# Forgetting attention by pairs of heads, with one 128 by 128 turn for each pair and block

## What is computed

```python
def forgetting_attention(q, k, v, f_logit, b_f):
    ...
    log_f = jax.nn.log_sigmoid(f_logit.astype(jnp.float32) + b_f.astype(jnp.float32))
    c = jnp.cumsum(log_f, axis=1).transpose(0, 2, 1)
    ...
    for blk in range(S // Q_BLOCK):
        q0, q1 = blk * Q_BLOCK, (blk + 1) * Q_BLOCK
        logits = jnp.einsum('bqhd,bkhd->bhqk', q[:, q0:q1], k[:, :q1]).astype(jnp.float32) * scale
        logits = logits + c[:, :, q0:q1, None] - c[:, :, None, :q1]
        ...
        p = jax.nn.softmax(logits, axis=-1)
        outs.append(jnp.einsum('bhqk,bkhd->bqhd', p.astype(v.dtype), v[:, :q1]))
```

## Time and profile before

| | |
|---|---|
| median of 3 runs | 3592.46 us |
| lowest and highest | 3590.16 and 3597.49 us |
| span of the profiled execution, first to last instruction | 3589.3 us |
| the profiled execution's own time, beside its span | not recorded; the lowest run is 0.9 us above the span |
| mean granted clock of TensorE | 0.997 of full speed |
| PE busy | 3512.9 us, 98% |
| PEld busy | 2764.4 us, 77% |
| DVE busy | 1567.7 us, 44% |
| ACT busy | 1279.2 us, 36% |
| POOL busy | 443.6 us, 12% |
| first score matmul of the stage of the change | 257.53 us |
| first matmul of the next stage on real data | 327.79 us |

### The profile page before, as it was taken

The page is one execution under the profiler, slowest core; times in us unless marked ns, Lnnn a source line. Parts: engine busy times, 40 slices in busy tenths (PEclk is TensorE's granted clock), DMA queues, the critical chain, the costliest instruction groups (busy, mean ns, idle before and its releaser), DMA issues. The chain is left out here.

```text
span 3589.3 us, 41664 instructions
## 1 busy us (share of the span) xinstructions
PE 3512.9 (98%) x15716; PEld 2764.4 (77%) x15740; DVE 1567.7 (44%) x2129; ACT 1279.2 (36%) x1792; POOL 443.6 (12%) x366
## 2 busy tenths in 40 slices
PE   9999999999999999999999999999999999999998
PEld 7787788877778886888875688877888875688886
DVE  3386433356643334333375733335333255733335
ACT  4343422245542324332333533235332333533324
POOL 0001111000111101221000022102221000022102
PEclk9999999999999999999999999999999999999999
DMA  4201233222123322333220233313333220133322
GB/s 146 87 1 36 81 95 110 96 71 71 38 80 99 105 95 65 95 100 105 84 64 15 71 96 97 112 61 98 100 94 109 79 78 18 53 94 99 111 71 76
DMA packets 78029, 292.06 MB, mean 81 GB/s; under 512 B 8656, under 2 KB 11472, under 8 KB 77648
## 3 DMA queue, kind: packets, MB, share of 16 engines
q1 hardware_dynamic: 77328, 289.31, 25.4%
q10 hardware_dynamic: 576, 1.05, 0.1%
HBM read 288.22 MB, written 2.10 MB: 81 GB/s over the span
## 5 line engine op out<-in xcount | busy, mean ns | idle before, releaser
L157 DVE TENSOR_TENSOR w_low<-w_raw,w_high 128x1024 fp32r<-128x1024 f32 (+4 forms) x513 | 672.6, 1311 | 1520.1 <-ACT w_high L152 1520.0
L191 PE MATMUL bank<-x_high,w_high 128*128 128x512 f32 x2856 | 1119.2, 392 | 21.0 <-DVE w_low L157 9.2
L193 PE MATMUL bank<-x_high,w_low 128*128 128x512 f32 x2856 | 1111.5, 389 | 0.0
L192 PE MATMUL bank<-x_low,w_high 128*128 128x512 f32 x2856 | 1111.4, 389 | 0.0
L152 ACT CAST w_high<-w_raw 128x1024 fp32r<-128x1024 f32 (+4 forms) x513 | 555.0, 1082 | 842.5 <-PE bank L193 835.4
L191 PEld LDWEIGHTS bank<-x_high,w_high 128*128 128x128 f32 x2856 | 536.2, 188 | 147.2 <-DVE w_low L157 14.3
L193 PEld LDWEIGHTS bank<-x_high,w_low 128*128 128x128 f32 x2856 | 536.1, 188 | 112.3
L192 PEld LDWEIGHTS bank<-x_low,w_high 128*128 128x128 f32 x2856 | 536.4, 188 | 111.2 <-issue 1.7
L191 PE MATMUL bank<-hidden_high,w_high 128*128 128x512 f32 x1056 | 410.8, 389 | 0.0
L192 PE MATMUL bank<-hidden_low,w_high 128*128 128x512 f32 x1056 | 410.8, 389 | 0.0
L193 PE MATMUL bank<-hidden_high,w_low 128*128 128x512 f32 x1056 | 410.8, 389 | 0.0
(11 more groups left out here) (537 smaller groups left out, 3432.5 us busy)
## 6 DMA issues: line engine op xcount, KB each, us to landing
w_raw<-in_stream SPq DMA_DIRECT2D x381, 512.0 KB, 3.5
w_raw<-in_stream SPq DMA_DIRECT2D x96, 704.0 KB, 4.0
w_raw<-in_stream SPq DMA_DIRECT2D x16, 384.0 KB, 3.1
w_raw<-in_stream SPq DMA_DIRECT2D x4, 576.0 KB, 3.7
dft_positions<-in_dft SPq DMA_DIRECT2D x2, 1024.0 KB, 4.8
w_raw<-in_stream SPq DMA_DIRECT2D x16, 128.0 KB, 2.1
out<-result SPq DMA_DIRECT2D x4, 512.0 KB, 2.7
h<-in_x ACTq DMA_DIRECT2D x4, 256.0 KB, 6.2
```

The lines of the kernel that those rows point to most:

```text
L157: self.nc.vector.tensor_tensor(self.lo[:, j % 2, 0:size], self.raw[:, j % RAW_SLOTS, 0:size], self.hi[:, j % 2, 0:size].bitcast(F32), ALU. ...
L191: nc.tensor.matmul(out, lhs[0], rhs[0], start=start, stop=False)
L192: nc.tensor.matmul(out, lhs[0], rhs[1], start=False, stop=False)
L193: return nc.tensor.matmul(out, lhs[1], rhs[0], start=False, stop=stop)
```

## The change

The units are put in another order and the turn is cut into smaller ones. `per` is 128 / 64 = 2 heads. The outer loop goes over pairs of heads, the next over blocks, and the inner one over the two heads of the pair. So units 0 and 1 have 512 keys, 2 and 3 have 384, 4 and 5 have 256, 6 and 7 have 128, and unit 8 starts again with 512 for the next pair of heads. After each second unit the 128 finished columns are turned by one transpose and copied by one ACT instruction of 128 by 128. That makes 16 turns of one transpose and 16 copies in place of 4 turns of four transposes and 4 copies.

`o_rows` shrinks from 2 x 512 to 2 x 128 columns. Turns 0 and 1 and all odd ones go to bank 6, the even ones from turn 2 on to bank 7. Since the first turn comes in iteration 4, the side task's logarithm and exponential go from ACT's iteration 4 to 3, PE waits for the logarithm in iteration 4 in place of 10, ahead of that iteration's scores, and it waits for DVE's multiplication in iteration 8.

```diff
--- before.py
+++ after.py
@@ -1462,8 +1462,13 @@
 
 
     blocks = range(NB - 1, -1, -1) if causal else range(NB)
-    units = [(qb, h) for qb in blocks for h in range(heads)]
+    per = P // width
+    units = [(qb, h) for first in range(0, heads, per) for qb in blocks for h in range(first, first + per)]
     n_units = len(units)
+
+    def turned_bank(i):
+
+        return C.bank[7 if i >= 2 and i % 2 == 0 else 6]
 
     def keys(n):
         return (units[n][0] + 1) * P if causal else T
@@ -1473,7 +1478,7 @@
             return ctx.enter_context(sbuf(nc, name, shape, F32))
         probs = sb("probs", [P, 2, T])
         probs_t = sb("probs_t", [P, 2, T])
-        o_rows = sb("o_rows", [P, 2, HALF_T * P])
+        o_rows = sb("o_rows", [P, 2, P])
         top = sb("top", [P, n_units])
         bias = sb("exp_bias", [P, n_units])
         total = sb("total", [P, n_units])
@@ -1515,15 +1520,13 @@
                                                   start=b == 0, stop=b == nk - 1)
                         mm.then_inc(S.summed_v, 1)
                     m = n - 3
-                    if m >= 0 and units[m][1] == heads - 1:
-                        i = m // heads
+                    if m >= 0 and m % per == per - 1:
+                        i = m // per
                         pe.wait_ge(S.normed, m + 1)
-                        if i >= 2:
-                            pe.wait_ge(S.o_used, i - 1)
-                        for f in range(HALF_T):
-                            mm = nc.tensor.transpose(C.bank[6 + i % 2][:, f * P:(f + 1) * P],
-                                                     o_rows[:, i % 2, f * P:(f + 1) * P], C.ident)
-                        mm.then_inc(S.o_turned, 1)
+                        if i:
+                            pe.wait_ge(S.o_used, max(1, i - 1))
+                        nc.tensor.transpose(turned_bank(i)[:, 0:P], o_rows[:, i % 2, :], C.ident
+                                            ).then_inc(S.o_turned, 1)
                     if n >= n_units:
                         keep_warm(nc, C, C.bank[0], (2, 2, 6)[n - n_units])
 
@@ -1540,12 +1543,11 @@
                     if side:
                         side.on_act(nc, C, act, S, n)
                     m = n - 4
-                    if m >= 0 and units[m][1] == heads - 1:
-                        qb, i = units[m][0], m // heads
+                    if m >= 0 and m % per == per - 1:
+                        (qb, h), i = units[m], m // per
                         act.wait_ge(S.o_turned, i + 1)
-                        nc.scalar.copy(dst[:, dst0:dst0 + HALF_T, qb * P:(qb + 1) * P],
-                                       C.bank[6 + i % 2][:, :].rearrange("p (f q) -> p f q", q=P)
-                                       ).then_inc(S.o_used, 1)
+                        nc.scalar.copy(dst[:, dst0 + h // per, qb * P:(qb + 1) * P],
+                                       turned_bank(i)[:, 0:P]).then_inc(S.o_used, 1)
 
             @block.vector
             def _(dve):
@@ -1566,7 +1568,7 @@
                                               C.bank[2 + m % 2][:, 0:keys(m)]).then_inc(S.turned_used, 1)
                     m = n - 2
                     if 0 <= m < n_units:
-                        i, h = m // heads, units[m][1]
+                        i, h = m // per, units[m][1]
                         dve.wait_ge(S.exp_done, m + 1)
                         nc.vector.reciprocal(inv[:, m:m + 1], total[:, m:m + 1]).then_inc(S.inv_ready, 1)
                         dve.wait_ge(S.inv_ready, m + 1)
@@ -1574,7 +1576,7 @@
                         at = h * width % P
                         if i >= 2:
                             dve.wait_ge(S.o_turned, i - 1)
-                        nc.vector.tensor_scalar(o_rows[:, i % 2, h * width:(h + 1) * width],
+                        nc.vector.tensor_scalar(o_rows[:, i % 2, at:at + width],
                                                 C.bank[4 + m % 2][:, at:at + width], inv[:, m:m + 1], None,
                                                 ALU.mult).then_inc(S.normed, 1)
                     if side:
@@ -1838,7 +1840,7 @@
         norm = C.rstd[:, :]
         if n == 1:
             nc.scalar.activation(norm, C.bank[7][:, :], ACT.Square).then_inc(S.squared, 1)
-        if n == 4:
+        if n == 3:
             act.wait_ge(S.var, 1)
             nc.scalar.activation(norm, C.bank[6][:, :], ACT.Ln, scale=1.0 / P, bias=C.eps[EPS]).then_inc(S.logged, 1)
             act.wait_ge(S.logged, 1)
@@ -1852,8 +1854,9 @@
         if n == 3:
             pe.wait_ge(S.squared, 1)
             nc.tensor.matmul(C.bank[6][:, :], C.ones, C.rstd[:, :], start=True, stop=True).then_inc(S.var, 1)
-        if n == HEADS + 2:
+        if n == 4:
             pe.wait_ge(S.logged, 1)
+        if n == 8:
             pe.wait_ge(S.y_step, 1)
 
     def on_dve(self, nc, C, dve, S, n):
```

## The result

The changed kernel takes 3599.06 us in the median of 13 runs (3595.75 to 3608.86), the kernel before 3592.46 (3588.45 to 3597.91). The ratio is 1.0020 with a 95% interval of 1.0013 to 1.0027: slower, by about what this kernel's measurement can just tell.

A forecast was written before the change was run, and what follows sets the result against it. PE, busy 98% of the span, was taken as the bound, so the change could only move its waits. Terms 2.4 - 0.7 + 0.1 + 0.1 + 0.3 - 0.1 - 0.45 = +1.7 gave 3594.2 us, range 3588.5 to 3600.5.

The forecast's parts named there:

- rival 1: The clock falls during PE's new wait for the logarithm: 6 us at half speed, +4.7, 3597.2 us; chance 0.2.
- the prediction's own signs: Expected in the profile: clock 1.00 behind the logarithm wait, no standing at turns, no later stage changed over a microsecond.
- The wait for the logarithm: PE stands ahead of unit 4's scores until ACT's logarithm ends, with nothing hiding it: +2.4 us.
- A: The start of unit 0's product with `v` on PE, from which the prediction counts times.
- The 0.7 that goes: PE's old loss at its transposes behind the side task's two table loads disappears: -0.7 us.
- DVE's part of the side task: DVE's side work stands between units 6 and 7 and delays unit 7's maximum: +0.1 us.
- The steps to 512 keys: Three steps from units of 128 to 512 keys, where short work covers a long chain: +0.1 us.
- The turns: Sixteen single transposes of finished rows cost PE more than four groups of four: +0.3 us.
- The order: Units of 128 keys no longer run together, as large units stand between them: -0.1 us.
- the rest of the end: At the stage's end, 0.23 more work during the last exponential's wait, -0.23, and turn 14 in the tail, +0.11.
- Rival 2: Each of 12 added turns waits for DVE's scaled rows: +6.6, with the rest +8.3, 3600.8 us; chance 0.05.
- Rival 3: ACT's table load runs beside its exponential, cutting the logarithm wait to 1.1: +0.4, 3592.9 us; chance 0.05.

The follow-up runs named there:

- e4: Kernel before, with only the logarithm moved to ACT's iteration 3 and PE's wait for it to iteration 4: 3595.81 us, ratio 1.0010.
- e2: Changed kernel with PE's wait for the logarithm moved to where a turn first writes bank 6: 3595.28 us, ratio 1.0002.
- e7: Kernel before, with one ACT table for logarithm and exponential loaded at the stage's start: 3591.70 us, ratio 0.9995.
- e8: e3 with one ACT table for logarithm and exponential loaded at the stage's start: 3592.86 us, ratio 0.9999.
- e6: e2 with one ACT table for logarithm and exponential loaded at the stage's start: 3592.25 us, ratio 1.0001.
- e1: Changed kernel with ten matmuls that compute nothing ahead of PE's wait for the logarithm: 3596.89 us, ratio 1.0006.
- e10: e4 with ten matmuls that compute nothing ahead of PE's wait for the logarithm: 3595.62 us, ratio 1.0008.
- e11: Changed kernel unaltered, run for a third profile: median 3595.61 us, ratio 1.0012; its profiled execution took 3603.93 us.
- e12: e6 with eleven matmuls that compute nothing ahead of PE's 2.58 us wait in the projection stage: 3591.32 us, ratio 0.9999.
- e5: Changed kernel with one ACT table for logarithm and exponential loaded at the stage's start: 3591.45 us, ratio 0.9997.
- e3: e2 with the units ordered by blocks as before, still sixteen turns of one transpose: 3592.56 us, ratio 0.9997.

## Why the prediction came out as it did

The measured 3599.06 lies in the range, 4.9 above the forecast, and it is neither clearly within 0.2% nor beyond it. That it lies there owes something to the width of the range, 12 us: it is nearer to rival 1's 3597.2 than to the forecast's 3594.2. By the prediction's own signs the forecast case did not happen, since the clock fell behind the logarithm.

- **The wait for the logarithm.** Predicted from A + 4.13 to A + 6.54; measured, with A at 264.98, A + 4.13 to A + 6.55. Right to 0.01, and e4 shows that it alone makes the loss.
- **The 0.7 that goes** The earlier trace rows did go, and came back in another form (0.30 + 1.18) as soon as the early wait was taken away in e2. It was hidden, not removed; e7 shows that it goes when the table loads go (-0.80 in the stage).
- **DVE's part of the side task**, +0.1: the scores of the first unit of 512 keys took 1.60 for 1.54. **The steps to 512 keys**, +0.1: no wait at any of the three. **The turns**, +0.3 with -0.33 at the end: e7 to e8 gives 0.0. **The order**, -0.1 and the rest of the end, -0.12: e8 to e6, which holds these two and the two terms of +0.1 as well, gives -0.36 where they add up to 0.0. The parts measured one by one, 2.4 - 0.8 + 0.0 - 0.4 = +1.2, agree with the 1.3 of e1; the prediction's sum was +1.7. Its bounds add up to +0.85 and +3.35; the +3.5 given is a slip and bears on nothing.
- **The step that failed is the weighing of rival 1.** The prediction put "the new wait, 2.4, ... on the side of the first" case, the wait of 2.58 behind which the clock held, and gave the fall a chance of 0.2. Ordering the cases by the length of the wait was the error, and the kernel before alone could have shown it: it has a second wait of 3.02 us at the same line, behind which the clock stayed at 1.00 (1859 to 1865), and low stretches also begin at 755.2, 1007.8 and 1383.3, at waits of only 0.86, 0.69 and 1.89.

```profile
1859.28 0.50 PE L191 MATMUL bank<-latent_high,w_high 128*128 128x512 f32 x1 [3.02 <-DVE mla_q L1382]
```

Over the profiles the clock fell behind the wait of 2.58 in 7 of 13, behind the two waits of 3.02 in 14 of 28, and behind the new one in all three of the changed kernel and in e4. Its price, 3.0 us, was also one outcome: e4 against e10 gives 3.0, e1 against the first profile 1.5, and e11 against e1 10.7. Even the counts of the old waits would have asked for a chance near one half, and behind the new one the fall was the rule.
- **Rival 2**, a wait at each turn, did not appear: of the changed kernel's 16 turns only the last has a wait for the scaled rows, 0.5, and the kernel before has the same. **Rival 3** did not either: the load stands behind the row sum.

## What to carry to other kernels

A wait should stand directly ahead of the instruction that needs it, and the same chain has to be followed on past that wait: what was hidden behind it comes next. A single profile tells one outcome of a clock that falls in some executions only, so look at the same wait in several profiles, and at whether the timed runs fall in groups with different mean clocks, before putting a chance on it. Where PE must wait for about 2 us among many small matmuls, matmuls that compute nothing are cheap insurance: here the clock held behind them in e1, e10 and e12, in one profile each. Removing what PE waits for is better, and here one table load at the start of the stage, while ACT waits anyway, replaced the two around the logarithm. A load that is gone is a gain only where PE waited for it: in the next stage one went and PE's time didn't move.

## What the runs showed of the hardware

- Once low, the clock stayed low for 3.4, 6.8 or 23.9 us behind waits of 2.2 to 2.3 us of idle PE, with no gap in PE's rows behind the wait. It fell 0.8, 0.4 and 0.3 us behind the end of the wait in the three profiles of the changed kernel (3.4, 3.4 and 23.9 us low) and 0.3 ahead of it in e4 (6.8). The three lengths occur in kernels that do the same kind of work there, transposes and products in float32. What decides between them stays open; the profiles don't show it. I didn't vary what PE does behind the wait.
- Two waits of 0.30 and 1.18 with work between them also came ahead of a low stretch (e2); waits of 0.75 (e5), 0.70 (the kernel before) and 0.60 (e3) did not, in one profile each. Elsewhere in the kernel before low stretches begin at waits of 0.69 (1007.8), 0.86 (755.2) and 1.89 (1383.3), so the length of the wait alone doesn't decide it.
- Between 126 executions of one kernel the time varied by 11 us, and the mean clock with it: 0.997 at 3588, 0.993 at 3599. Low stretches near 9 and near 152 us, ahead of the stage, came together or not at all in the 13 profiles without the fill there, and moved the stage's start by 1.3 to 2.2 us between profiles of identical code.
